# Gates of three token tiles made in one pass over the gate weights, with the gates of two tiles parked in DRAM

## The reference, cut to what matters

```python
h = rms(x)
cq, ckv, kpe, bq, bk, bv, iq, iw, ik, ga, gb = split(h @ w_in)      # ga, gb: 1024 columns each
o_a = latent_attention(cq, ckv, kpe)                                 # mixer A, 8 heads
o_b = sparse_attention(bq, bk, bv, iq, iw, ik)                       # mixer B, top-k keys by an indexer
x = x + (sigmoid(ga) * (o_a @ w_o_a) + sigmoid(gb) * (o_b @ w_o_b)) @ w_out
x = x + peer(rms(x))       # 8 heads; each token gathers 128 rows of u and of v out of 16384 experts
```

## Time and profile before

| what | value |
|---|---|
| median of 3 runs | 1927.01 us (1926.09 to 1929.76) |
| the profiled execution, its own time | 1926.13 us |
| its span | 1924.3 us |
| TensorE busy / granted clock | 67% / 0.75 |
| VectorE busy | 69% |
| ScalarE busy | 30% |
| GpSimd busy | 27% |
| moved by DMA | 704.92 MB |
| first dot of the loop starts | 310.2 us |

### The profile page before, as it was taken

The page is one execution under the profiler, slowest core; times in us unless marked ns, Lnnn a source line. Parts: engine busy times, 40 slices in busy tenths (PEclk is TensorE's granted clock), DMA queues, the critical chain, the costliest instruction groups (busy, mean ns, idle before and its releaser), DMA issues.

```text
span 1924.3 us, 25838 instructions
## 1 busy us (share of the span) xinstructions
PE 1298.7 (67%) x8684; PEld 715.0 (37%) x8684; DVE 1325.8 (69%) x3948; ACT 575.3 (30%) x2040; POOL 522.0 (27%) x552
## 2 busy tenths in 40 slices
PE   7779884766887757577986766769877534444344
PEld 3447752234444432244553422446544211111111
DVE  3644228688886656789876666899866577686754
ACT  2223202342332222433431323324422222222222
POOL 0000003233332231333332323322322333333332
PEclk9878986967878878778888868778889755555555
DMA  5042348999999999999999999999999999999997
GB/s 205 6 135 78 122 151 334 414 423 426 425 423 424 400 413 418 409 425 425 367 425 422 423 424 391 423 425 351 384 424 422 425 426 426 427 426 424 427 422 313
DMA packets 121653, 704.92 MB, mean 366 GB/s; under 512 B 18224, under 2 KB 21344, under 8 KB 51376
## 3 DMA queue, kind: packets, MB, share of 16 engines
q0 software_dynamic: 78336, 570.46, 71.1%
q1 hardware_dynamic: 38672, 129.26, 17.5%
q10 hardware_dynamic: 4512, 3.54, 0.6%
HBM read 700.13 MB, written 3.02 MB: 365 GB/s over the span
## 4 chain that ended last, share of the span: by engine, by line
DMA 34%; DVE 21%; PE 21%; issue 16%; ACT 3%; POOL 1%; DVEq 0%; POOLq 0%
DMA rows<-in_peer_uv,index 25%; DVE rows L2043 9%; PE ps_v L1397 5%; DMA wch<-in_w_row 4%; PE ps_f L1104 2%; PE ps_f L1241 2%; DMA wch<-in_w_out 2%; PE ps_h L1377 2%; PE ps_f L1270 2%; DMA wch<-in_peer_wq 2%; PE ps_f L1291 1%; POOL rows L1081 1%; DMA wch<-in_keyb 1%; DVE score L1819 1%; PE ps_f L1256 1%
## 5 line engine op out<-in xcount | busy, mean ns | idle before, releaser
L1081 POOL DMA_INDIRECT rows<-in_peer_uv,index x544 | 520.2, 956 | 1285.9 <-PE ps_v L1397 1007.1
L2043 DVE CUSTOM_DVE_ANT_0 rows<-rows,ps_h 128x1024 f32<-128x1024 f32 x544 | 658.0, 1220 | 290.4 <-DMA rows<-in_peer_uv,index 217.0
L1397 PE MATMUL ps_v<-rows,diag 128*32 128x256 f32 x4352 | 431.9, 512 | 457.7 <-ACT diag L1651 440.9
L1397 PEld LDWEIGHTS ps_v<-rows,diag 128*32 128x32 f32 x4352 | 127.8, 133 | 711.2 <-ACT diag L1651 575.0
L1642 ACT ACTIVATE tan<-arg 128x2 f32<-128x2 f32 x272 | 55.5, 204 | 872.3 <-DVE arg L2053 838.5
L1645 ACT ACTIVATE weight<-tan,lead 128x1 f32<-128x1 f32 x544 | 180.8, 379 | 9.1
L1651 ACT ACTIVATE diag<-sel,weight 128x32 f32<-128x32 f32 x544 | 140.7, 305 | 0.0
L1241 PEld LDWEIGHTS ps_f<-bufh,wch 128*128 128x128 f32 x768 | 117.1, 239 | 22.7 <-issue 20.5
L1241 PE MATMUL ps_f<-bufh,wch 128*128 128x128 f32 x768 | 123.6, 328 | 0.0
L1104 PE MATMUL ps_f<-wch,bufh 128*128 128x512 f32 (+1 forms) x192 | 83.6, 574 | 30.6 <-DMA wch<-in_w_row 27.7
L1291 PE MATMUL ps_f<-bufh,wch 128*128 128x128 f32 x384 | 55.7, 305 | 11.7 <-DMA wch<-in_peer_wq 10.6
(11 more groups left out here) (319 smaller groups left out, 1740.4 us busy)
## 6 DMA issues: line engine op xcount, KB each, us to landing
wch<-in_w_gate SPq DMA_DIRECT2D x64, 512.0 KB
wch<-in_w_row SPq DMA_DIRECT2D x39, 512.0 KB
wch<-in_w_o SPq DMA_DIRECT2D x32, 512.0 KB
wch<-in_w_out SPq DMA_DIRECT2D x32, 512.0 KB
wch<-in_peer_wq SPq DMA_DIRECT2D x32, 512.0 KB
rows<-in_peer_uv,index POOLq DMA_INDIRECT x544
w_tok<-in_w_tok SPq DMA_DIRECT2D x4, 1640.0 KB, 13.6
wch<-in_keyb SPq DMA_DIRECT2D x6, 512.0 KB
```

The lines of the kernel that those rows point to most:

```text
L1081: pool.indirect_dma_start(rows[c % RING][:, :, :].rearrange("p a d -> p (a d)"), None, io.peer_uv[:, :], at).then_inc(s_uv[c % RING], 16)
L1397: ins = nc.tensor.matmul(ps_v[GROUP * a:GROUP * (a + 1), :], diag[:, c % DRING, :], rows[c % RING][:, 1, QD * a:QD * (a + 1)], start=False ...
L2043: v.tensor_tensor_reduce(out=u, in0=u, in1=ps_h[:, :], scale=1.0, scalar=0.0, op0=ALU.mult, op1=ALU.add, accum_out=dots[:, c % KEEP:c % KE ...
```

## The change

In pass 1 (tile 1) the raw rows of tiles 2 and 3 are loaded too, normalised and turned into columns, so that one buffer, `trio`, holds the columns of tiles 1, 2 and 3. The gates are then made for all three tiles with matmuls 384 columns wide (`gates_of_three`), one gate at a time in bank 3, each evicted on its own by two tanh (`tanh_of_three`): tile 1's part goes to `sg`, the part of tiles 2 and 3 to a two-slot buffer `stage` (in the space of `qh`), from which SP writes it to a DRAM tensor `keep_g`. Passes 2 and 3 load no gate weights and make no gates; each reads its tile's 1 MB from `keep_g` into `sg`. The small DMAs for `vm` go out from GpSimd's queue and the loads of `key0` from SP's.

```diff
-    m.buf_h = pl("bufh", [P, DC, P])
+    m.trio = pl("trio", [P, 3, D])
+    m.buf_h = m.trio[:, 0, :].rearrange("p (c k) -> p c k", c=DC)
...
-    m.xb = [pl(f"xb{i}", [P, D]) for i in range(2)]
-    m.hrows = [pl(f"hrows{i}", [P, D]) for i in range(2)]
+    m.xb = [m.trio[:, 2, :], pl("xb1", [P, D])]
+    m.hrows = [m.trio[:, 1, :], pl("hrows1", [P, D])]
...
+    stage = m.qh[:, :, :].rearrange("p (s a i) k -> p s a (i k)", s=2, a=2)
...
-    loads = [(p, j) for p in range(NP)
-             for j in (list(range(J_AT, V_AT + 1)) + list(range(CHUNKS)) if p else range(K_AT))]
+    loads = [(0, j) for j in range(K_AT)]
+    loads += [(p, j) for p in range(1, NP)
+              for j in list(range(J_AT, V_AT + 1)) + list(range(G_AT if p == 1 else Z_AT, CHUNKS))]
... SP queue
                     for n in range(13):
                         load(p, J_AT + n, io.w_row[n, :, :])
+                        if p == 1 and n == WRING - 1:
+                            sp.wait_ge(s_h, 1)
+                            sp.dma_start(raw(3, True), io.x_prompt[P * 2:P * 3, :]).then_inc(s_xe[0], 16)
+                            sp.wait_ge(s_xc, 1)
+                            sp.dma_start(raw(4, True), io.x_prompt[P * 3:P * 4, :]).then_inc(s_xe[1], 16)
...
+                    if p >= 2:
+                        sp.wait_ge(s_new, 16 * 5 * p)
+                        sp.wait_ge(s_pairc, 3 * p)
+                        sp.wait_ge(s_qk, p)
+                        for a in range(2):
+                            sp.wait_ge(s_keep[a], 8 * DC)
+                        sp.dma_start(sg[:, :, :, :], io.keep_g[p - 2, :, :, :, :]).then_inc(s_sgl, 16)
+                        load_x(i)
...
+                if p == 1:
+                    for n in range(WRING, 2 * DC + DC):
+                        if n < 2 * DC:
+                            load_gate(p, n)
+                        else:
+                            load(p, Z_AT + n - 2 * DC, io.w_o[n - 2 * DC, :, :])
+                        if n % 2 == 1 and (n - 5) // 2 < DC:
+                            j = (n - 5) // 2
+                            sp.wait_ge(s_sig, DC * p + j + 1)
+                            sp.dma_start(io.keep_g[:, :, :, j, :].rearrange("i p a k -> p a i k"),
+                                         stage[:, j % 2, :, :].rearrange("p a (i k) -> p a i k", i=2)).then_inc(s_keep[j % 2], 16)
+                        if n == 2 * DC + WRING - 1:
+                            sp.wait_ge(s_wu[slot_of(p, G_AT + 2 * DC - 1)], uses_of(p, G_AT + 2 * DC - 1))
+                            load_x(members[0])
... TensorE
+            def gates_of_three(j, a):
+                if a == 0:
+                    if j == 0:
+                        pe.wait_ge(s_ht, 2 * nth_x(4, True))
+                    pe.wait_ge(s_sig, DC + j)
+                else:
+                    pe.wait_ge(s_half, j + 1)
+                w = use(1, G_AT + 2 * j + a)[:, :].rearrange("p (c k) -> p c k", c=DC)
+                for k in range(DC):
+                    ins = nc.tensor.matmul(ps_f[:, 3, 0:3 * P].rearrange("p (i k) -> p i k", i=3), w[:, k, :],
+                                           trio[:, :, k, :], start=(k == 0), stop=(k == DC - 1))
+                ins.then_inc(s_wu[slot_of(1, G_AT + 2 * j + a)], 1)
...
+                        if p == 1 and x in (8, 11):
+                            turn_x(i + (x - 5) // 3, True)
...
-                    if x := gate_at(p, k):
+                    if p == 0 and (x := gate_at(p, k)):
                         gate(p, *x)
+                    if p == 1 and (x := gate_at(p, k)):
+                        gates_of_three(*x)
... ScalarE
+            def tanh_of_three(j, a):
+                last_w = G_AT + 2 * j + a
+                act.wait_ge(s_wu[slot_of(1, last_w)], uses_of(1, last_w))
+                if j == 0 and a == 0:
+                    act.wait_ge(s_new, 16 * 5)
+                if j >= 2 and a == 0:
+                    act.wait_ge(s_keep[j % 2], 16 * (j // 2))
+                nc.scalar.activation(sg[:, a, j, :], ps_f[:, 3, 0:P], ACT.Tanh, scale=0.5)
+                nc.scalar.activation(stage[:, j % 2, a, :], ps_f[:, 3, P:3 * P], ACT.Tanh, scale=0.5).then_inc(s_sig if a else s_half, 1)
...
+                        if p == 1 and x in (6, 9):
+                            root_x(i + (x - 3) // 3, True)
... VectorE
+                        if p == 1 and x in (5, 8):
+                            x_sum(i + (x - 2) // 3, True)
+                        if p == 1 and x in (7, 10):
+                            x_scale(i + (x - 4) // 3, True)
+                        if p == 1 and x in (9, 12):
+                            x_columns(p, i + (x - 6) // 3, True)
... start: from ScalarE's queue to GpSimd's (vm) and SP's (key0)
-                act.dma_start(vm[here, 0, cols], m.va_of(4)[DEC:DEC + META, h, :]).then_inc(s_vm, 16)
-                act.dma_start(vm[here, 1, cols], m.vb_of(4)[DEC:DEC + META, :]).then_inc(s_vm, 16)
+                pool.dma_start(vm[here, 0, cols], m.va_of(4)[DEC:DEC + META, h, :]).then_inc(s_vm, 16)
+                pool.dma_start(vm[here, 1, cols], m.vb_of(4)[DEC:DEC + META, :]).then_inc(s_vm, 16)
...
-                act.dma_start(key0[:, r, :], io.keyb[r, :, :]).then_inc(s_key0, 16)
+                        sp.dma_start(key0[:, r, :], io.keyb[r, :, :]).then_inc(s_key0, 16)
```

More of the change, by code:

```diff
@@ L849, in scored, with raw, column_rows, nth_x @@
         return ps_f[0:q, u % 2, 0:nk]
+    def raw(i, early=False):
+        return xin if not early else hrows[0] if i == 3 else xb[0]
+    def column_rows(i, early=False):
+        return trio[:, i - 2 if early else 0, :, :]
+    def nth_x(i, early=False):
+        return i - 1 if early or i == 2 else i + 1
     def earlies(i, u):
@@ L922, in stream @@
         s_xin = sem("s_xin")
+        s_xe = [sem(f"s_xe{a}") for a in range(2)]
+        s_half = sem("s_half")
+        s_keep = [sem(f"s_keep{a}") for a in range(2)]
+        s_sgl = sem("s_sgl")
         s_gt = sem("s_gt")
@@ L1047, in _ @@
                         load_x(i)
-                for n in range(WRING, 2 * DC):
-                    load_gate(p, n)
-                for j in range(DC):
-                    load(p, Z_AT + j, io.w_o[j, :, :])
+                    for r in range(2):
+                        sp.dma_start(key0[:, r, :], io.keyb[r, :, :]).then_inc(s_key0, 16)
+                if p == 0:
+                    for n in range(WRING, 2 * DC):
+                        load_gate(p, n)
+                    for j in range(DC):
+                        load(p, Z_AT + j, io.w_o[j, :, :])
+                if p == 1:
+                    for n in range(WRING, 2 * DC + DC):
+                        if n < 2 * DC:
+                            load_gate(p, n)
+                        else:
[8 more added lines that the diff above has]
+                            load_x(members[0])
+                if p >= 2:
+                    for j in range(WRING, DC):
+                        load(p, Z_AT + j, io.w_o[j, :, :])
                 for k in range(DC):
@@ L1068, in _ @@
                            allow_small_or_imprecise_dtypes=True).then_inc(s_num, 1)
+            pool.wait_ge(s_zero, 1)
+            for h in range(H):
+                here, cols = slice(META * h, META * (h + 1)), slice(AV * h, AV * (h + 1))
+                pool.dma_start(vm[here, 0, cols], m.va_of(4)[DEC:DEC + META, h, :]).then_inc(s_vm, 16)
+                pool.dma_start(vm[here, 1, cols], m.vb_of(4)[DEC:DEC + META, :]).then_inc(s_vm, 16)
             for c in range(NCOL):
@@ L1248, in blend @@
                     pe.wait_ge(s_otc, 2 * (PASSES[p][-1] + 1))
-                if j == 1:
+                if j == 1 and p < 2:
                     pe.wait_ge(s_sig, DC * (p + 1))
@@ L1606, in front @@
                         relu(*x)
-                    if (x := tanh_at(p, k)) is not None:
+                    if p == 0 and (x := tanh_at(p, k)) is not None:
                         tanh_gates(p, x)
+                    if p == 1 and (x := gate_at(p, k - 1)):
+                        tanh_of_three(*x)
                     if k == at.turn + 1:
@@ L1664, in block_out @@
                     act.dma_start(dst[:, QD * a:QD * (a + 1)], yo[GROUP * a:GROUP * (a + 1), n % 2, :]).then_inc(s_out[n % 2], 16)
-            act.wait_ge(s_zero, 1)
-            for h in range(H):
-                here, cols = slice(META * h, META * (h + 1)), slice(AV * h, AV * (h + 1))
-                act.dma_start(vm[here, 0, cols], m.va_of(4)[DEC:DEC + META, h, :]).then_inc(s_vm, 16)
-                act.dma_start(vm[here, 1, cols], m.vb_of(4)[DEC:DEC + META, :]).then_inc(s_vm, 16)
-            for r in range(2):
-                act.dma_start(key0[:, r, :], io.keyb[r, :, :]).then_inc(s_key0, 16)
             for _ in front(0):
```

63 lines of the change are left out of this document (39 added, 24 removed).

## The result

The changed kernel takes 1939.31 us (median of 20 runs, 1926.51 to 1948.16); the kernel before, run beside it, takes 1929.02 us (median of 20, 1922.69 to 1933.33). The ratio is 1.0049, with a 95% interval of 1.0033 to 1.0066. So the change makes the kernel half a per cent slower, where 1905 us were forecast. The profiled execution took 1940.5 us, with a span of 1938.7.

What follows compares the result with a forecast made beforehand. DMA transfers were taken to set the loop's pace, with VectorE nearly level in the middles; −11.8 + 20 − 15 − 14 = −21 us against 1926.1, with the runs' median 0.9 above, gave 1905 us, range 1883 to 1925.

Steps and rivals of the forecast that it cites:

- The start, −11.8: Pass 0: moving small DMA issues off ScalarE removes TensorE's whole 11.80 us wait for the first relu.
- Rival D: Start: the move gives nothing because something else holds pass 0; 1917 us, chance 0.07.
- The transfers, −29 net: Passes 1 to 3: gate loads removed, less added transfers; +9.7 us in pass 1, −19.4 in each of 2 and 3.
- My price of 7 us: Pass 1: cost of writing 2.10 MB of kept gates in 512-byte runs, between bounds of 5.0 and 10.5 us.
- Rival A: All passes: transfers decide everywhere, so the saved bytes show in full; 1885 us, chance 0.22.
- Pass 1, +20: Pass 1 lengthens: 2.7 us for x loads, 7 for kept-gate writes, 10.5 for TensorE's excess in the middle.
- three slow ones: Pass 1's middle: 3 of 16 wide gates at the half clock, so gates take 102 us.
- the 7.5 us that I let the ring bank: Pass 1's middle: three gathers of 2.5 us run ahead, softening TensorE's excess, given back in the stretch behind.
- Rival C: Pass 1's middle: TensorE keeps its idle time and clock mix, taking 231 us; total 1946 us, chance 0.09.
- Passes 2 and 3, −15 and −14: Middles: VectorE's waits shrink (−11, −9) and the ring banks half the further DMA saving (−4, −5).
- rival B: Middles: VectorE already the limit, ring banks nothing, passes 2 and 3 give only 8.9 us; 1920 us, chance 0.19.
- the signs of being wrong that I had named: VectorE's middles not shortening, pass 1's diagonal waits staying at 28 us, or 512-byte-run writes costing over 10 us.

Runs made afterwards that it cites:

- experiment 3: Kernel before the change, with only the vm issues moved to GpSimd and the key0 loads to SP: 1920.84 us, ratio 0.9951.
- experiment 1: Changed kernel plus eight unread 128x128 matmuls at each of the 16 ticks of passes 2 and 3 where a gate once ran: 1925.77 us, ratio 0.9988.
- experiment 2: Changed kernel with pass 1's gates 128 columns wide, for tile 1 only, all transfers kept: 1924.87 us, ratio 0.9984.
- experiment 5: Kernel of experiment 1 with the middle's 50 ticks spread over 64 columns instead of 54: 1936.97 us, ratio 1.0047.
- Experiments 7 and 8: Mixer B's top-key searches left out in passes 2 and 3, in the kernels of experiment 1 (1897.88 us) and experiment 3 (1902.33 us).
- experiment 10: Changed kernel with the edits of experiment 1 and experiment 2 together: 1917.10 us, ratio 0.9929.
- experiment 4: Kernel before the change, with one of eight products in each gate of passes 2 and 3, loads kept: 1930.66 us, ratio 1.0029.

## Why the prediction was wrong, by its own steps

**The start, −11.8: right in mechanism, in size perhaps too large.** The wait of the earlier trace rows is gone; it gave 8.5 us of span in the changed kernel and 9.5 us (6 to 13) by the ratio of experiment 3. What became late next is the load of the first gate (2.02 us of waiting), a thing I should have looked for. The rule of the Trainium skill ("DMA: Bandwidth & Descriptors", "Issuing engines are not separate DMA queues"), that issuing from another engine saves only a small time, would have given nothing; here the issue time was on the path and the measurement decides. Rival D falls.

**The transfers, −29 net: right in bytes, not in time.** SP's queue moves 10.5 MB less, as forecast, and takes 22.7 us less of the engines, where I said some 26. My price of 7 us for the writes of 512-byte runs was not tested by itself. Of the 19.4 us that passes 2 and 3 were each to need less, only 4.5 and 4.0 show as time, and those only with the clock given back (experiment 1 against 3). Rival A, by which all of it would show, falls; the DMA engines were not full in these middles.

**Pass 1, +20: the sum and its two parts were right, the working inside in part luck.** The pass as a whole lengthened by 20.6 us. With narrow gates (experiment 2) it takes 405.6 us in place of 414.4, and 393.8 before the change (one trace each): 8.8 us go with the gates' width, where I had 10.5 for TensorE, and 11.8 stay, where I had 9.7 for the transfers. Inside TensorE's part, the terms were off against each other. I had TensorE at 181 us in the middle and it was busy for 159.9. Of the 21 us between, 9 are gates, 92.7 us in place of 102: four gates had a slow part, but none was slow throughout. The other 12 are the rest of its work, 67.2 us in place of 79.1: I had carried over its times at a clock of 0.81, and the clock was 0.93; some 35 of its matmuls also fell behind the middle. The rule that activity releases the throttle ("TensorE: Matmul & The Clock Gate", Part 1 of the Trainium skill), by which all sixteen would take 89 us, was nearer than my count of three slow ones. Against it, the middle kept 10.6 us of TensorE idle, which I had covered with backlog, and the 7.5 us that I let the ring bank and give back didn't come: the stretch behind the middle grew by 3.3 us and the one ahead by 2.5. Rival C, whose place this was, needed a middle of 211 us or more; it took 170.5. The change came out slower, but not by rival C.

**Passes 2 and 3, −15 and −14: the step that failed.** Measured were −6.8 and +8.9. Two things were wrong in it.

The first is rival B, to which I gave 0.19. I had VectorE's waits for TensorE halve and its waits for rows go, and let the ring bank half of what the transfers had to give beyond that. (The waits come to 10.3 us in pass 2, where I wrote 11; the −15 stands either way.) Almost none of it came: with the clock given back (experiment 1) the middles still stand at 161.0 and 168.4 us. VectorE's waits for TensorE there are 9.6 us in pass 2 and 12.3 in pass 3, where they were 9.9 and 11.4; its waits for rows fell only from 5.3 to 4.0 and from 3.6 to 2.0. VectorE's 86 to 88% in the earlier trace rows was already about as much as it reaches: in experiment 5 its share stays at 87% when the same units are spread over more columns, and the highest in any trace is 90%. I had seen this row and read 87% as "13% free". Experiments 7 and 8 show where the 39 us of transfers went: 1.2 us of them show in the middle of pass 2 with VectorE's work as it is, 10.6 when it is lighter. In all, 8.5 us show in passes 2 and 3 (experiment 1 against 3), most of it behind the middles; less what the transfers added in pass 1 cost, about 4 us are left in the whole time, and those are not shown.

The second was no part of any rival: that matmuls taken away make the others slower. I wrote "gates of 41.7 us leave TensorE" and counted that as time it could not lose. In fact these gates were what kept its clock at 0.82 to 0.84. Without them it fell to 0.58 and 0.56, scores and mixes took 29 and 38% longer, and the chain from gather through mix, score and logit stretched: TensorE was busier in pass 3 than before. Experiments 1 and 10 show this for the changed kernel, where it costs 11 to 12 us, most of it in pass 3; experiment 4 shows the fall of the clock in the kernel before, with little time lost. The forecast for the changed middles said DMA shares below 0.97, and this held (0.94, 0.87); but it does not mean what I took it for: the loop waits, and the engines idle for want of requests. Of the signs of being wrong that I had named, the first came true: VectorE's middles did not shorten.

**The sum by the runs.** Start −9.5 us (experiment 3), wide gates about +12 (2 and 10), clock about +11 (1 and 10), transfers and all else about −4 (10 against 3): +10, which is the measured 0.49%. That they meet is no proof: the same four ratios (the changed kernel, experiments 2, 10 and 3) give both the parts and the whole, so they must add up; what they tell is the size of each part. My prediction had −11.8 for the start, +20 for pass 1 and −29 for passes 2 and 3, and no term for the clock.

**What stays open.** Why VectorE's share stops near 87 to 90% is not fully taken apart: a quarter of its idle time is in waits too short to be listed, and neither the number of slots in the ring nor `LAG` was varied. Why the gates' matmuls keep the clock up and the scores and mixes do not is open as well. The clock's effect on pass 2 isn't clear: 161.4 us at 0.58 and 161.0 at 0.81, but 157.2 at 0.92 in one trace, and 165.3 at 0.77 in that of experiment 10. Why 235 matmuls fewer cost the kernel before at most 2 us a middle (experiment 4) and the changed one 10 in pass 3 is open too; the trace of the changed kernel has the lower clock of the two in pass 3, 0.56 against 0.67. And the changed kernel scatters more than the kernel before, 21.7 us against 10.6 over 20 runs each.

## What to carry to other kernels

Matmuls taken off TensorE have a price if it was they that kept its clock up: look at the granted clock of the stretch, and at what the matmuls that stay would cost at the lower level, before you count them as saved. Adding idle matmuls in their place is a cheap way to find out. An engine that is busy for 87% of a stretch in which it passes work to and fro may be at its limit. A stretch where DMA and such an engine are both nearly full gives little to whoever relieves only one, so saved bytes are to be priced by the stretch in which they would have moved.

## What the runs showed of the hardware

- TensorE's clock stayed mostly at the lower level while the engine was busy for 85% of a stretch (152.16 of 179.3 us, granted clock 0.56), and stood at 0.84 with 141.00 of 168.4 us, 84%. A busy share does not tell the clock. Eight matmuls of 128x128 in a row, sixteen times in a middle, made the difference. That more activity releases the throttle is the Trainium skill's rule too ("TensorE: Matmul & The Clock Gate", Part 1), and the direction agrees.
- On TensorE's timeline in the slow stretch, matmuls follow each other with hardly a gap, four scores in 2.13 us, eight mixes in 1.08 us, and the clock doesn't rise (eight mixes take 0.64 us in the middle of pass 1, at a clock of 0.93):

```profile
1311.42 2.13 PE L1236 MATMUL ps_f<-kt,bufq 96*128 96x264 f32 x4
1313.48 1.08 PE L1479 MATMUL ps_v<-rows,diag 128*32 128x256 f32 x8
1314.49 1.97 PE L1281 MATMUL ps_f<-va,probT 128*128 128x64 f32 x8
```

- Issues of small DMAs took 0.48 us each on GpSimd, 0.61 on ScalarE. The writes of kept gates, in runs of 512 bytes, took 16.7 us from issue to landing for 256 KB, the reads back 8.8 us for 1 MB, medians and both beside the gathers:

```profile
keep_g<-qh SPq DMA_DIRECT2D x8, 256.0 KB, 16.7
...
sg<-keep_g SPq DMA_DIRECT2D x2, 1024.0 KB, 8.8
```
